# A decoder trunk on one core: RMS scale moved behind the products, h split piece by piece, router operands swapped

## The reference, cut to what matters

```python
xn = rmsnorm(h, mix_norm[i]);  u = xn @ w_in[i]          # q k v lx lg ga gb
q = head_rms(q, q_norm[i]);    k = head_rms(k, k_norm[i])
h = h + (sigmoid(ga) * (attn @ W_pa) + sigmoid(gb) * (lru @ W_pb)) @ w_out[i]
xn2 = rmsnorm(h, ffn_norm[i])
h = h + swiglu(xn2, ...)      if i == 0 else h + moe_ffn(xn2, ...)   # top 2 of 8 experts
xn3 = rmsnorm(h, ple_norm[i])
h = h + sigmoid(xn3 @ ple_gate_w[i]) * (p[i] @ ple_proj_w[i])
```

## Time and profile before

| what | value |
|---|---|
| median of 3 runs | 1978.64 us (1976.98 to 1979.96) |
| the profiled execution | 1977.99 us; span 1976.1 us |
| granted TensorE clock, mean | 0.974; from 293 to 305 us (norm 1) 0.91 |
| busy DVE, ACT | 1488.7 us (75%), 1191.0 us (60%) |
| PE's longest waits beside the one below | attention bias L1319, 27.6 us in 25 waits; weight splits L441, 20.2 in 4; squares L573, 12.4 in 4; y copy L732, 12.0 in 1 |
| HBM | 483.15 MB read, 245 GB/s over the span |

### The profile page before, as it was taken

The page is one execution under the profiler, slowest core; times in us unless marked ns, Lnnn a source line. Parts: engine busy times, 40 slices in busy tenths (PEclk is TensorE's granted clock), DMA queues, the critical chain, the costliest instruction groups (busy, mean ns, idle before and its releaser), DMA issues. The chain is left out here.

```text
span 1976.1 us, 29743 instructions
## 1 busy us (share of the span) xinstructions
PE 1852.5 (94%) x10906; PEld 1621.5 (82%) x10907; DVE 1488.7 (75%) x2029; ACT 1191.0 (60%) x1601; POOL 2.4 (0%) x15
## 2 busy tenths in 40 slices
PE   6988898999988989888999999999999999999977
PEld 5866898999987868887888888888888888888867
DVE  7585776555557774947988989889898998988954
ACT  4546643333434558326777777777777777777742
POOL 0000000000000000000000000000000000000000
PEclk8999998999999999988999999999999999999988
DMA  7332352535524323525988989889799898998950
GB/s 287 124 115 111 122 204 113 229 129 219 207 86 147 120 86 129 193 91 201 376 349 342 380 308 384 341 335 385 305 380 373 311 378 307 377 375 310 384 193 22
DMA packets 36789, 485.40 MB, mean 246 GB/s; under 512 B 4048, under 2 KB 6368, under 8 KB 7136
## 3 DMA queue, kind: packets, MB, share of 16 engines
q1 hardware_dynamic: 34272, 481.93, 63.6%
q10 hardware_dynamic: 2432, 2.31, 0.4%
HBM read 483.15 MB, written 1.07 MB: 245 GB/s over the span
## 5 line engine op out<-in xcount | busy, mean ns | idle before, releaser
L1593 DVE TENSOR_TENSOR w_lo<-raw,w_hi 128x1024 fp32r<-128x1024 f32 x672 | 775.8, 1219 | 73.4 <-ACT w_hi L743 72.6
L743 ACT ACTIVATE w_hi<-raw 128x1024 fp32r<-128x1024 f32 x672 | 665.0, 1054 | 104.6 <-DMA raw<-in_moe_w 66.6
L441 DVE TENSOR_TENSOR w_lo<-raw,w_hi 128x1024 fp32r<-128x1024 f32 x236 | 283.8, 1221 | 147.0 <-ACT w_hi L436 140.1
L845 PE MATMUL work<-w_hi,bias_r 128*128 128x512 f32 x896 | 356.8, 398 | 4.3 <-DVE w_lo L1593 4.3
L847 PE MATMUL work<-w_hi,bias_r 128*128 128x512 f32 x896 | 350.3, 391 | 0.0
L845 PE MATMUL work<-x_r,w_hi 128*128 128x256 f32 x1088 | 324.9, 299 | 26.6 <-DVE x_r L1201 16.2
L846 PE MATMUL work<-w_lo,bias_r 128*128 128x512 f32 x896 | 349.9, 390 | 0.0
L846 PE MATMUL work<-x_r,w_hi 128*128 128x256 f32 x1088 | 314.6, 289 | 0.0
L847 PE MATMUL work<-x_r,w_lo 128*128 128x256 f32 x1088 | 314.1, 289 | 0.0
L436 ACT ACTIVATE w_hi<-raw 128x1024 fp32r<-128x1024 f32 x236 | 243.1, 1052 | 107.2 <-PE work L847 55.6
L845 PEld LDWEIGHTS work<-x_r,w_hi 128*128 128x128 f32 x1088 | 215.2, 198 | 38.1 <-issue 30.5
(11 more groups left out here) (270 smaller groups left out, 2290.1 us busy)
## 6 DMA issues: line engine op xcount, KB each, us to landing
raw<-in_moe_w SPq DMA_DIRECT2D x168, 2048.0 KB, 9.7
raw<-in_mix_w SPq DMA_DIRECT2D x34, 2048.0 KB, 8.2
raw<-in_dense_w SPq DMA_DIRECT2D x21, 2048.0 KB, 8.3
raw<-in_ple_w SPq DMA_DIRECT2D x4, 2048.0 KB, 10.8
areaK<-in_ple_p SPq DMA_DIRECT2D x2, 1024.0 KB, 9.5
hT<-in_xT SPq DMA_DIRECT2D x1, 1024.0 KB, 5.4
gate_a<-bias_line ACTq DMA_DIRECT2D x1, 1024.0 KB, 6.8
areaB<-bias_line ACTq DMA_DIRECT2D x1, 1024.0 KB, 9.2
```

Source lines behind the costliest of these rows:

```text
L441: eng.tensor_tensor(unit(w_lo, g), raw_part(g), unit(w_hi, g).bitcast(F32), ALU.subtract).then_inc(split_ok, 1)
L743: act.activation(w_hi[u][:, :], raw[n % RING][:, (i % 4) * QUARTER:(i % 4 + 1) * QUARTER], ACT.Copy).then_inc(hi_ok, 1)
L845: pe.matmul(out, stat[0], move[0], start=start, stop=False, skip_group_check=True)
L1593: dve.tensor_tensor(w_lo[u][:, :], raw[n % RING][:, (i % 4) * QUARTER:(i % 4 + 1) * QUARTER], w_hi[u][:, :].bitcast(F32), ALU.subtract).th ...
```

## The change

The inputs of the products are no longer normalised first. ACT writes `hi` as the rounding of h * gain straight from each piece of h (an activation with the gain column as scale), DVE writes `lo = h * gain - hi` for each piece, both as soon as the piece is final: inside the out products, the last down product, the embedding, and the add of the last expert. DVE adds the squares of the pieces, so that PE needs one matmul with ones (and two with one column of ones, for tokens as rows) in place of eight, and does it behind the first group of the stage it belongs to (`norm_root`), in q/k/v behind the second quarter. The root's reciprocal then multiplies results: `up` in the dense layer (both halves, before silu), the gate product in `ple`, v, the squares and the reciprocal in q/k norms, the token rows and the logits in routing. For lx, gb, ga and lg the normalised input is still made (`renorm`, `renorm_lo`), during q/k/v. Further: the last down product runs bank by bank; the embedding has four banks, and its first four embedding matmuls stand ahead of the first gate product; the logits come with the router's 8 columns stationary and xnT moving, and are transposed back; the pick matrix of expert 0 is built ahead of the gates; an expert's gathered tokens are taken behind the second split of its own job in place of the end of the job before; on DVE no weight split stands ahead of `decays()`.

```diff
+            def norm_piece(n, k):                       # ACT
+                wait_h(act, n, k)
+                dst = xnT if routed(n) else (h_hi if n % 3 == 0 else xn_hi)
+                act.activation(dst[:, k, :], hT[:, k, :], ACT.Copy, scale=gain_of(n)[:, k:k + 1]).then_inc(h_rounded, 1)
+                if k % 2:
+                    act.activation(sq, hT[:, k - 1:k + 1, :], ACT.Square).then_inc(squared, 1)
 ...
+            def norm_root(n):                           # PE
+                pe.wait_ge(squares_added, n + 1)
+                sums = squares_of(n)
+                if n % 3 == 0 or routed(n):
+                    for tt in range(TT):
+                        mm = pe.matmul(pv_ps[:, tt:tt + 1], sums[:, tt * P:(tt + 1) * P], ones[:, 0:1], start=True, stop=True)
+                if not routed(n):
+                    mm = pe.matmul(misc[:, 0:T], ones[:, :], sums[:, 0:T], start=True, stop=True)
 ...
+            def norm_lo(n, k):                          # DVE
+                dve.wait_ge(h_rounded, KT * n + k + 1)
+                dve.scalar_tensor_tensor(out=low[:, k, :], in0=hT[:, k, :], scalar=gain_of(n)[:, k:k + 1],
+                                         in1=hi[:, k, :].bitcast(F32), op0=ALU.mult, op1=ALU.subtract).then_inc(normed, 1)
+            def norm_sum(n, q):
+                if q:
+                    step(dve.tensor_tensor(sq[:, 0:2 * T], sq[:, 0:2 * T], sq[:, 2 * T * q:2 * T * (q + 1)], ALU.add))
+                if q == 3:
+                    dve.tensor_tensor(sq[:, 0:T], sq[:, 0:T], sq[:, T:2 * T], ALU.add).then_inc(squares_added, 1)
+            def norm_root(n):
+                    ins = dve.reciprocal(rinv_col, rms_col)
+                    ins = dve.reciprocal(rinv[:, :], squares_of(n)[:, 2 * T:3 * T])
+            def renorm(l, ks): ...     # xnT = hT * gain * rinv, rounded by ACT, then renorm_lo on DVE
 ...
             def qk_norm(l):                             # DVE (ACT alike)
-                    lo.to(phase_q[(l, "mix")] + 4 * c + 9)
+                    lo.to(phase_q[(l, "mix")] + 4 * c + (6 if i == 0 else 9))
+                    if i == 0:
+                        norm_root(3 * l)
+                        renorm(l, range(0, 4))
+                    if i == 1:
+                        renorm_lo(l, range(0, 4))
+                        renorm(l, range(4, 8))
+                    if i == 2:
+                        renorm_lo(l, range(4, 8))
 ...
             def qkv(l):                                 # PE
+                        if c == 0 and q == 1:
+                            norm_root(3 * l)
 ...
             def dense(l):                               # DVE
+                    wait_full(dve, l, "ffn", c, ft)
+                    taken(dve.tensor_tensor(up, bank_of(l, "ffn", c, ft).rearrange("p (h t) -> p h t", h=2),
+                                            rinv[:, :].unsqueeze(1).to_broadcast([P, 2, T]), ALU.mult), l, "ffn", c, ft)
 ...
             def ple(l):                                 # DVE
+                    dve.tensor_tensor(s, bank_of(l, "ple", j)[:, 0:T], rinv[:, :], ALU.mult).then_inc(ple_scaled, 1)
+                    if l + 1 < DEPTH and j >= 2 and j % 2 == 0:
+                        norm_piece(3 * l + 3, j // 2 - 1)
 ...
             def moe(l):                                 # PE
+                    mm = pe.matmul(misc[0:EXPERTS, 0:T], rw[:, k, :], xnT[:, k, :], start=(k == 0), stop=(k == KT - 1))
-                        mm = pe.matmul(misc[:, 8 * tt:8 * tt + 8], xnT[:, k, tt * P:(tt + 1) * P], rw[:, k, :],
 ...
                 for i in range(JOB_Q):                  # ACT (DVE: split_gathered)
+                    if i == 2:
+                        take_gathered(j + first)
-                take_gathered(j + (first + 1))
 ...
-            norm(0)
+            for q in range(4):
+                norm_piece(0, q)
             decays()
```

More of the change, by code:

```diff
@@ L125, in trunk @@
     own = {g: (2 + TT * (g[2] - 1) + g[3], g[0]) for g in groups if g[1] == "qkv" and g[2]}
-    place = {g: (i % 2, i // 2) for i, g in enumerate(g for g in groups if g not in own)}
-    place.update(own)
+    own.update({g: (g[2] % 4, None) for g in groups if g[1] == "ple"})
+    place, used, turn = {}, [0] * 6, 0
+    for g in groups:
+        if g in own:
+            b = own[g][0]
+        else:
+            b, turn = turn % 2, turn + 1
+        place[g] = (b, used[b])
+        used[b] += 1
     at = {}
@@ L698, in mixer @@
                     taken(ins, l, "lg", j)
-                hi.to(phase_q[(l, "ffn")] + 5)
+                for k in range(KT):
+                    hi.to(phase_q[(l, "mix")] + 60 + k + 6)
+                    norm_piece(3 * l + 1, k)
             def dense(l):
@@ L847, in split_product @@
                 return pe.matmul(out, stat[1], move[0], start=False, stop=stop, skip_group_check=True)
-            def norm(n):
-                for k in range(KT):
-                    if k % 2 == 0:
-                        pe.wait_ge(squared, 4 * n + k // 2 + 1)
-                    mm = pe.matmul(misc[:, 0:T], ones[:, :], squares[:, k, :], start=(k == 0), stop=(k == KT - 1))
+            def norm_root(n):
+                pe.wait_ge(squares_added, n + 1)
+                sums = squares_of(n)
+                if n % 3 == 0 or routed(n):
+                    for tt in range(TT):
+                        mm = pe.matmul(pv_ps[:, tt:tt + 1], sums[:, tt * P:(tt + 1) * P], ones[:, 0:1], start=True, stop=True)
+                if not routed(n):
+                    mm = pe.matmul(misc[:, 0:T], ones[:, :], sums[:, 0:T], start=True, stop=True)
                 mm.then_inc(summed, 1)
@@ L1024, in ple, with embed @@
                 pe.wait_ge(ple_in, 32 * (l + 1))
-                for j in range(KT):
+                def embed(j):
                     out = group_open(l, "ple", j)
@@ L1029, in ple @@
                         pe.matmul(out[:, T:2 * T], wpp[:, k, j * P:(j + 1) * P], p_sb[:, k, :], start=(k == 0), stop=(k == 1))
+                for j in range(4):
+                    if j >= 2 and l % 2 == 0:
+                        pe.wait_ge(h_ffn, 4 * (l // 2) + j - 1)
+                    embed(j)
+                for j in range(KT):
+                    if j >= 4:
+                        embed(j)
+                    out = bank_of(l, "ple", j)
                     g = phase_q[(l, "ple")] + j
@@ L1416, in mixer @@
                     taken(dve.tensor_tensor(hT[:, j, :], hT[:, j, :], bank_of(l, "out", j)[:, 0:T], ALU.add), l, "out", j)
-                    bk, n = place[(l, "out", j)]
-                    dve.wait_ge(work_free[bk], n + 1)
-                    dve.sem_inc(h_mixed, 1)
+                    if j % 2 and j > 1:
+                        norm_piece(3 * l + 1, j // 2 - 1)
+                norm_piece(3 * l + 1, 3)
             def dense(l):
@@ L1466, in routing @@
                 rb = row[:, R_RB:R_RB + EXPERTS].unsqueeze(1).to_broadcast([P, TT, EXPERTS])
-                dve.wait_ge(logits_done, 1)
+                step(dve.memset(gate_m, 0.0))
+                step(dve.memset(rank_m, 0.0))
                 dve.wait_ge(pool_route, 3)
-                step(dve.tensor_tensor(L, misc[:, 0:16].rearrange("p (t e) -> p t e", t=TT), rb, ALU.add))
+                dve.wait_ge(logits_turned, 1)
+                for tt in range(TT):
+                    step(dve.scalar_tensor_tensor(out=L[:, tt, :], in0=misc[:, T + EXPERTS * tt:T + EXPERTS * (tt + 1)],
+                                                  scalar=rinv_col[:, tt:tt + 1], in1=rb[:, tt, :], op0=ALU.mult, op1=ALU.add))
                 step.settle()
```

360 lines of the change are left out of this document (227 added, 133 removed).

## The result

The changed kernel took 1931.01 us (median of 4 runs, 1930.66 to 1931.10) against 1977.81 us for the kernel before on the same chip (4 runs, 1976.73 to 1979.96): ratio 0.9762, 95% interval 0.9745 to 0.9779. The prediction was 1934, range 1923 to 1948. The profiled spans are 1929.2 and 1976.1 us, so -46.9 against a sum of -44.9.

A forecast was written before the change was run, and what follows sets the result against it. TensorE, busy 1852.5 of 1976.1 us, bounds the kernel; its idle time around the RMS norms can be won. Terms +6.8, -12.2, -14.4, -0.5, -13.1, -11.5 sum to -44.9: 1978.64 becomes 1934 us, range 1923 to 1948.

The forecast's parts named there:

- Mixer to dense: From the mixer's last out product into the dense layer: TensorE's stream nearly unbroken, root hidden, -12.2 us.
- Dense to embedding: From the dense layer's last down product through the per-layer embedding's gate products: pieces split under other products, -14.4 us.
- Embedding to mixer 1: From the last gate product to layer 1's q/k transposes: VectorE late and then the bound, gain given back, -0.5 us.
- Rivals 1 and 2: q/k/v stages cost more (-34, 1945 us, 17%); or less, VectorE not late out of the embedding (-55, 1924 us, 16%).
- rival 4: Whole kernel: only the waits move, VectorE takes back what the norms free, 1978 us; chance 3%.
- Start: Kernel start to layer 0's q/k transposes: first q/k/v product at 26.6 instead of 19.40, +6.8 us, bounds 0 and +11.
- Routing: Mixer 1's end to first expert product: shorter logits and root chain, products at 20.35 instead of 33.4, -13.1 us.
- Tail: Last combine to the end: VectorE puts pieces between the adds, so the last products start earlier, -11.5 us.
- Experts: Expert jobs: nothing changes on TensorE though gathered tokens are taken at another point, zero.
- rival 3: Expert jobs: ScalarE waits for the gather, TensorE runs dry, 6.6 us x 8 = 53 us, 1987 us; chance 4%.
- the sum of -42: Whole kernel by the skill's 2.66 us table switch: root chains at start and mixer 1 each about 1.4 us longer.

The follow-up runs named there:

- early evacuation: Changed kernel with ScalarE evacuating the first lx product (in layer 0 also two bias copies) ahead of the last two q/k/v groups: 1923.04 us, ratio 0.9724.
- early split: Changed kernel with VectorE making the low parts of the first four weight pieces ahead of the decays: 1919.67 us, ratio 0.9711.

## Why the prediction was right, point by point

- **Mixer to dense, -12.2; measured -12.0.** The unbroken stream at 300.34 to 300.46 is what was worked out, and undoing either half (scale +9.5, split +3.9) brings most or part of the loss back.
- **Dense to embedding, -14.4; measured -13.5.** Of the missing 0.9, 0.6 is the four embedding pairs: 3.3 us (544.06 to 547.33) where 2.7 were charged.
- **Embedding to mixer 1, -0.5; measured +0.4.** This stretch gives its gain back, as worked out: squares complete at +8.8 (9.0 charged), a wait of 3.16 (3.6 charged), then lx 0 behind the last root. The early evacuation gets 3.4 of it back. Rivals 1 and 2, which had +3 and -5.5 us on this stretch, are both out, and so is rival 4, which had the whole gain come back.
- **Start, +6.8; measured +6.5.** Right in size, but by two errors of 2 us that cancel, which is luck. The exponential, charged at 21.3, ran at 18.96 (no table load stood ahead of it), so the first product came at 24.61 and not at 26.6, and VectorE's last q/k group ended at 72.5, where the chain was charged to 74.7. From there to the transposes it took 12.7 us where 10.8 were charged: PE had just waited 3.00 us for ScalarE's copy of the bias, and the granted clock behind that wait was 0.54 (71.70 to 75.00), which the sum has no term for. The chain through the q/k groups is the bound, as charged: from column reciprocal to last group it takes 39 us in the changed kernel (33.28 to 72.51) and with the early split (26.37 to 65.25). It only begins sooner there, so what was lost was the order at the start. Stated as "the decays ahead of the first split", the step was right.
- **Routing, -13.1; measured -12.5.** The size is right, one share of it was put down to the wrong cause. I counted the swap of the router's operands as 6.84 us replaced by 3.6. The router with its old operands takes 3.64 at full clock: those 3.2 us came from the gap that went.
- **Tail, -11.5; measured -13.0.** VectorE's adds, pieces and squares are done 11.1 us after the combine, as charged (11.3), but its last weight splits begin at once behind them (11.0, where 12.6 was charged), and the second product starts 12.3 us after the combine, not 13.9.
- **Experts, 0; measured -1.4**, made of -1.7 for the moved taking of the tokens (0.24 between two gathers, seven times; the first job shows nothing of it), -0.55 for less half clock at the first products, and +0.9 from the last gather to the last combine, where PE's wait for the y copy grew from 12.0 to 12.8. A term of zero was wrong by a small amount in the good direction; rival 3 needed +6.6 a job.
- **The root's table.** ScalarE at norm 4 after the change:

```profile
852.61 1.28 ACT L620 ACT_TABLE_LOAD   x1
853.91 0.20 ACT L620 ACTIVATE small<-small 128x1 f32<-128x1 f32 x1
```

The next activation starts 0.02 us behind the load's end. The Trainium skill ("ScalarE: Activation LUTs", section "What ACT_TABLE_LOAD costs") adds a drain and comes to 2.66 us for a switch; the trace disagrees here as it did before the change, and the sum of -42 by that rule was the wrong one.

## What to carry to other kernels

A factor that is one number for each token belongs behind the product wherever the chain that makes it (sum, root, reciprocal; putting it back cost 4 to 10 us a norm here) stands between two streams of matmuls. It pays twice, for the chain and for the half clock behind the gap. But split the input piece by piece too, or the helpers' queues take back part of the gain (13 of 47 us here); and after such a change read the orders again in which the helpers stand: here two steps moved on VectorE's and ScalarE's queues brought another 15 us.

Before an operation gets the credit for a shorter time, compare its clock in both traces. Two forms of a product that differed by 3.2 us differed in nothing but the gap ahead of them. And taking away 4.9 us of waits brought 8.3 here, with the products behind them back at full clock.

## What the runs showed of the hardware

- 32 fp32 records with 128 stationary columns and 8 moving ones take 3.64 us at a granted clock of 1.00 and 6.84 at 0.54. 16 records with 8 stationary columns and 256 moving take 3.62. So for this product it made no difference on which side the small operand was.
- A rounding of 128x256 with a gain column as scale takes 0.51 us on ScalarE alone and 0.89 to 0.91 for two in a row; 0.47 each was charged.
- Behind waits of PE of 3.00 and 3.52 us in the changed kernel the granted clock was 0.54 and 0.58; at the same places without the first and with 1.58 us of the second it was 1.00.
- The same kernel, profiled twice, differed by 2.4 us in span, 1.6 of it in one stretch behind the gather where the granted clock was 0.72 in one profile and 1.00 in the other. For gains of about 1 us on this kernel the anchors near the edit say more than the total.
